# A two-layer transformer step on one core: the order of work at five norm boundaries, two modulation sums and the spatial gating

## What is computed

```python
for i in range(2):
    mod = c_act @ ada_w[i] + ada_b[i]                       # six vectors of 1024 for each layer
    sh1, sc1, g1, sh2, sc2, g2 = split(mod, 6)
    h = rmsnorm(x, norm_g[i, 0]) * (1.0 + sc1) + sh1
    y = mlstm_mixer(h, ...) if i == 0 else sgu_mixer(h, ...)
    x = x + g1 * rmsnorm(y, norm_g[i, 1])
    h = rmsnorm(x, norm_g[i, 2]) * (1.0 + sc2) + sh2
    y = square(relu(h @ ffn_w1[i])) @ ffn_w2[i]
    x = x + g2 * rmsnorm(y, norm_g[i, 3])
...
def sgu_mixer(h, ...):
    u, v = split(gelu(h @ w_in + b_in), 2)
    v = layernorm(v)
    sv = einsum('gts,bnsgc->bntgc', tril(ws), v in groups) + bs    # 16 groups of 128 features
    return (u * sv) @ w_out
```

## Time and profile before

| | us |
|---|---|
| median of three runs | 2238.09 |
| lowest and highest of them | 2231.41 and 2239.53 |
| the profiled execution's own time | 2227.2 |
| its span in the trace | 2225.4 |
| what lies around the span | 1.8 |

### The profile page before, as it was taken

One profiled execution on the slowest core, in us unless ns is written; L12 is line 12 of the kernel. 1 busy time (PEld: TensorE's weight loads), 2 busy tenths in 40 slices (PEclk: granted clock), 3 DMA queues, 4 the chain that ended last, 5 costly groups with the idle time before them and its releaser, 6 DMA issues.

```text
span 2225.4 us, 29809 instructions
## 1 busy us (share of the span) xinstructions
PE 2123.7 (95%) x11614; PEld 1777.6 (80%) x11614; DVE 1230.6 (55%) x1994; ACT 826.0 (37%) x1229; POOL 95.9 (4%) x71
## 2 busy tenths in 40 slices
PE   6999879999999999999999999999999999999997
PEld 5897768888888998788888888886666689888886
DVE  4666667666667445647333336535557756535455
ACT  3433334334244322325342343336445534424243
POOL 0000010000001002401000000100000000000000
PEclk9999989999999999999999999999999999999999
DMA  9451314666551432231223323222012131222221
GB/s 293 152 190 48 110 56 159 203 210 196 194 188 59 151 96 91 79 114 57 76 95 95 112 91 96 63 69 85 1 48 77 47 112 60 94 95 94 95 85 67
DMA packets 224630, 239.34 MB, mean 108 GB/s; under 512 B 6642, under 2 KB 219021, under 8 KB 223877
## 3 DMA queue, kind: packets, MB, share of 16 engines
q1 hardware_dynamic: 182757, 193.73, 27.1%
q10 hardware_dynamic: 41760, 44.06, 6.0%
HBM read 230.81 MB, written 6.31 MB: 107 GB/s over the span
## 4 chain that ended last, share of the span: by engine, by line
PE 66%; issue 18%; DVE 7%; DMA 3%; ACT 3%; DVEq 1%; POOL 1%; SPq 1%; ACTq 0%; POOLq 0%
PE bank L546 43%; PE bank L1133 4%; PE bank L686 2%; DMA ada_raw<-in_ada_w 2%; PE bank L740 2%; PE bank L644 2%; DVE ada_acc L1722 2%; PE bank L1081 1%; PE bank L1070 1%; PE bank L1028 1%; PE bank L1058 1%; PE bank L1104 1%; PE bank L1116 1%; ACT w_hi L1201 1%; PE bank L611 1%
## 5 line engine op out<-in xcount | busy, mean ns | idle before, releaser
L1711 DVE TENSOR_TENSOR w_lo<-raw,w_hi 128x2048 fp32r<-128x2048 f32 x137 | 314.6, 2296 | 246.2 <-ACT w_hi L1201 246.1
L546 PE MATMUL bank<-h_hi,w_hi 128*128 128x512 f32 x1056 | 413.7, 392 | 0.0
L546 PE MATMUL bank<-h_hi,w_lo 128*128 128x512 f32 x1056 | 411.7, 390 | 0.0
L546 PE MATMUL bank<-h_lo,w_hi 128*128 128x512 f32 x1056 | 411.6, 390 | 0.0
L1201 ACT ACTIVATE w_hi<-raw 128x2048 fp32r<-128x2048 f32 x147 | 280.1, 1905 | 314.4 <-PE bank L546 308.1
L546 PE MATMUL bank<-g_hi,w_hi 128*128 128x512 f32 x688 | 271.3, 394 | 9.4 <-DVE g_lo L2498 5.1
L546 PE MATMUL bank<-g_hi,w_lo 128*128 128x512 f32 x688 | 269.6, 392 | 0.0
L546 PE MATMUL bank<-g_lo,w_hi 128*128 128x512 f32 x688 | 269.4, 392 | 0.0
L546 PEld LDWEIGHTS bank<-h_hi,w_lo 128*128 128x128 f32 x1056 | 198.7, 188 | 41.6
L546 PEld LDWEIGHTS bank<-h_lo,w_hi 128*128 128x128 f32 x1056 | 198.8, 188 | 41.1 <-issue 0.2
L546 PEld LDWEIGHTS bank<-h_hi,w_hi 128*128 128x128 f32 x1056 | 198.7, 188 | 40.7 <-issue 0.2
(11 more groups left out here) (415 smaller groups left out, 3668.9 us busy)
## 6 DMA issues: line engine op xcount, KB each, us to landing
raw<-in_ffn_w SPq DMA_DIRECT2D x64, 1024.0 KB, 5.2
ada_raw<-in_ada_w ACTq DMA_DIRECT2D x40, 1024.0 KB, 5.2
raw<-in_w_up SPq DMA_DIRECT2D x22, 1024.0 KB, 5.0
raw<-in_b_w_in SPq DMA_DIRECT2D x16, 1024.0 KB, 5.3
raw<-in_w_in SPq DMA_DIRECT2D x15, 1024.0 KB, 5.6
raw<-in_a_w_in SPq DMA_DIRECT2D x12, 1024.0 KB, 5.5
ada_head<-in_ada_w SPq DMA_DIRECT2D x8, 1024.0 KB, 11.8
raw<-in_b_w_out SPq DMA_DIRECT2D x8, 1024.0 KB, 5.2
```

The lines of the kernel that those rows point to most:

```text
L546: mm = pe.matmul(o, x, y, start=(k == 0 and j == 0), stop=(k == kc - 1 and j == 2))
L1711: dve.tensor_tensor(w_lo[s][:], raw[s][:], f32(w_hi[s][:]), ALU.subtract).then_inc(sem("split_done"), 1)
```

## The change

It has three parts.

**The boundaries.** In `last_pair` the sums and spreads of half 0 come earlier: `sums` at k = 3 of block 0 of the second half (was k = 5), the first `spread_half` at k = 7 of block 0 (was k = 2 of block 1), the two batches of `x_sums` behind block 1 and at k = 2 of block 2 (were behind block 2 and at k = 2 of block 3), the second `spread_half` at k = 6 of block 2 (was k = 7 of block 3). The fourth square of y is no longer added by DVE; PE sums it by itself from its own tile. `first_pair` runs half 0 with k outside and the four blocks inside (was two tiles one after the other), with the norm steps of half 1 at k = 1, 2, 4, 5, 6 and 7. `merge` takes blocks in pairs, with one addition of 512 columns for two, and POOL adds nothing more. DVE and ACT get a new order for all of this; among it, the low part of the second tile of the next phase is made in one piece ahead of `y_out` of block 2 (it was in two pieces behind `y_out` of block 3), and on ACT the high part stands ahead of the squares of blocks 1 to 3 (it was ahead of that of block 3 alone). out2 gets the shared parts of this.

**The modulation.** Pieces 16 and 17 are summed inside the mixer, behind chunks 0 and 1; their loads, and that of 18, are issued there. 18 and 19 are summed in the two a_out tiles, and `last_ada` waits for the bias alone.

**The gating.** The turned weights come two tiles earlier, the norm of v skips ahead of some low parts, and the 16 groups stand in fours behind each of the last four b_in blocks, on four banks. ACT rounds the gated groups only behind its last gelu. The first b_out tile runs with k outside and its two blocks inside.

```diff
@@ TensorE, last_pair
-                            if (half, m, k) == (1, 0, 5):
-                                sums(0, 9 * kb_, sqa)
-                            if (half, m, k) == (1, 1, 2):
-                                spread_half(0, 2 * kb_)
-                            if two and (half, m, k) == (1, 3, 2):
-                                x_sums(name, 0, range(4, KB))
-                            if two and (half, m, k) == (1, 3, 7):
-                                spread_half(0, 2 * kb_ + 1)
+                            if (half, m, k) == (1, 0, 3):
+                                sums(name, 0)
+                            if (half, m, k) == (1, 0, 7):
+                                spread_half(name, 0)
+                            if two and (half, m, k) == (1, 2, 2):
+                                x_sums(name, 0, (2, 3))
+                            if two and (half, m, k) == (1, 2, 6):
+                                spread_half(name, 0, True)
...
-                        if two and (half, m) == (1, 2):
-                            x_sums(name, 0, range(4))
+                        if two and (half, m) == (1, 1):
+                            x_sums(name, 0, (0, 1))
@@ TensorE, sums
+                for i, sq in enumerate([sqa, T[3]]):
+                    if i == 0:
+                        pe.wait_ge(sem(f"sq_ready{half}"), 5 * kb_ + 1)
+                    else:
+                        pe.wait_ge(sem("y_squared"), 12 * kb_ + 8 + 4 * half)
@@ TensorE, first_pair
+                for k in range(KB):
+                    norm_step(name, k)
+                    pe.wait_ge(sem("h_ready0"), 8 * BOUNDS[name] + k + 1)
+                    for m in range(4):
+                        step(0, m // 2, m % 2, k, bank[m], True)
@@ TensorE, around a_out
+            for i in range(2):
+                ada_mm(16 + i, i)
             pe.wait_ge(sem("mix_out"), 8 + 2)
             for i in range(2):
                 tile(t0 + i, i % 2, q0 + i // 2, g_hi, g_lo)
-                ada_mm(16 + i, i % 2)
+                ada_mm(18 + i, i)
...
             def last_ada():
-                for i in range(2, 4):
-                    ada_mm(16 + i, i % 2)
                 pe.wait_ge(sem("ada_added"), 1)
@@ TensorE, gating
-            pe.wait_ge(sem("ws_masked"), 4)
-            pe.wait_ge(sem("v_normed"), NC)
-            for g in range(NSGU):
-                if g >= 2:
-                    pe.wait_ge(sem("sgu_added"), g - 1)
...
+            def sgu(t, b):
+                i = 2 * (t - t0 - 14) + b
+                if i == 0:
+                    pe.wait_ge(sem("ws_masked"), 4)
+                    pe.wait_ge(sem("v_normed"), NC)
+                for g in range(4 * i, 4 * i + 4):
+                    if g >= 4:
+                        pe.wait_ge(sem("sgu_added"), g - 3)
...
+            for s in range(2):
+                tile(t0 + 14 + s, s, q0 + 7, h_hi, h_lo, after_block=sgu)
@@ ScalarE, boundary
                 split_next(0)
-                for m in range(3):
-                    y_square(m, y[m], hs[0])
-                split_next(1)
-                y_square(3, y[3], hs[0])
+                y_square(0, y[0], hs[0])
+                split_next(1)
+                for m in range(1, 4):
+                    y_square(m, y[m], hs[0])
@@ VectorE, boundary
                 y_out(0, 0)
                 rest_of(t2, 0, next_w[name][0], 1)
                 y_out(0, 1)
                 y_sum(0, 0)
+                rest_of(t2, 1, next_w[name][1], 1)
+                y_out(0, 2)
                 y_sum(0, 1)
-                y_out(0, 2)
                 y_sum(0, 2)
                 y_out(0, 3)
-                y_sum(0, 3)
-                rest_of(t2, 1, next_w[name][1], 2, lambda: variance(0, 9 * kb_ + 1))
-                diagonal(0, 2 * kb_)
-                spread_done(0, 2 * kb_)
+                variance(0)
+                diagonal(0)
+                spread_done(0)
...
+                    for i in range(4):
+                        merge(0, i)
+                    y_out(1, 0)
+                    y_out(1, 1)
                     y_sum(1, 0)
+                    variance(0, True)
...
@@ VectorE, mixer
+                    ada_sum(16, 0, ada_raw, (sem("ada_in"), 16 * 9))
                 if c == 1:
                     w_rest(4, 1)
+                    ada_sum(17, 1, ada_raw, (sem("ada_in"), 16 * 10))
@@ VectorE, gating
-                if g == 2:
-                    w_rest(u0 + 7, 1)
-                if 3 <= g <= 10:
-                    sgu_rest(g - 3)
+                if g == 7:
+                    w_rest(u0 + 7, 0)
+                if g >= 11:
+                    sgu_rest(g - 11)
+            for g in range(5, 8):
+                sgu_rest(g)
+            w_rest(u0 + 7, 1)
```

More of the change, by code:

```diff
@@ new lines, in x_sums @@
+            def x_sums(name, half, pairs):
+                kb_, o = BOUNDS[name], bank[norm_banks(name, half)[2]]
+                for i in pairs:
+                    pe.wait_ge(sem(f"sq_ready{half}"), 5 * kb_ + i + 2)
+                    for b in (2 * i, 2 * i + 1):
+                        for c in range(2):
+                            mm = pe.matmul(o[:, c:c + 1], xsq[:, b, c * P:c * P + P], ones[:, 0:1],
+                                           start=(b == 0 and c == 0), stop=(b == KB - 1 and c == 1), skip_group_check=True)
@@ L665, in first_pair, with norm_step, step @@
+            def norm_step(name, k):
+                if k == 1:
+                    sums(name, 1)
+                if k == 2:
+                    spread_half(name, 1)
+                if k in (4, 5):
+                    x_sums(name, 1, (k - 4,))
+                if k == 6:
+                    x_sums(name, 1, (2, 3))
+                if k == 7:
+                    spread_half(name, 1, True)
             def first_pair(name, t, q):
-                one_bank = name == "out2"
-                for half in range(2):
+                def step(half, s, b, k, o, last):
@@ L689, in first_pair @@
-                    if half == 0 and not one_bank:
-                        spread_half(1, 2 * BOUNDS[name] + 1)
+                    wh, wl = (w[:, k * 256 + b * P:k * 256 + b * P + P] for w in next_w[name][s])
+                    for j, (x, y) in enumerate([(wh, h_hi[:, k, hs]), (wh, h_lo[:, k, hs]), (wl, h_hi[:, k, hs])]):
+                        mm = pe.matmul(o[:, hs], x, y, start=(k == 0 and j == 0), stop=(k == KB - 1 and j == 2))
+                    if k == KB - 1 and last:
+                        mm.then_inc(sem("block_done" if half else "half_done"), 1)
@@ L977, in _ @@
+            for i in range(1, 6):
                 first = i < 4
                 tile(t0 + i, i % 2, q0 + i // 2, h_hi if first else g_hi, h_lo if first else g_lo,
-                     ready=[(sem("sgu_split"), 0 if first else 8)] if i in (0, 4) else None)
+                     ready=[(sem("sgu_split"), 8)] if i == 4 else None)
             last_pair("b_out", t0 + 6, q0 + 3, g_hi, g_lo)
@@ L1858, in boundary @@
                 if two:
-                    merge(0, range(KB))
-                    for m in range(3):
-                        y_out(1, m)
+                    for i in range(4):
+                        merge(0, i)
+                    y_out(1, 0)
+                    y_out(1, 1)
                     y_sum(1, 0)
+                    variance(0, True)
                     y_sum(1, 1)
-                    variance(0, 9 * kb_ + 9, 1)
-                    y_sum(1, 2)
-                    diagonal(0, 2 * kb_ + 1)
@@ L1867, in boundary @@
[L1867 to L1874 removed]
+                    diagonal(0, True)
@@ new lines, in boundary @@
+                    h_rest(0, 4)
+                    diagonal(1)
+                    h_rest(0, 5)
+                    spread_done(1)
+                    merge(1, 0)
+                    merge(1, 1)
+                    h_scale(0, 6)
+                    h_rest(0, 6)
+                    merge(1, 2)
+                    merge(1, 3)
+                    h_scale(0, 7)
+                    h_rest(0, 7)
+                    variance(1, True)
+                    diagonal(1, True)
+                    spread_done(1, True)
```

354 lines of the change are left out of this document (187 added, 167 removed).

## The result

| | before | after |
|---|---|---|
| median of eight runs each, us | 2230.8 | 2221.0 |
| lowest and highest | 2228.03 and 2239.53 | 2215.22 and 2222.61 |
| span of the profiled execution | 2225.4 | 2213.4 |

The ratio of after to before is 0.9943 (95% interval 0.9930 to 0.9955). Of 2230.8 us that is 12.7 us less (10.0 to 15.6); the forecast was 17.5 less. That the median landed within half a microsecond of the forecast time is partly luck: with eight runs the median of before is 2230.8, not 2238.09.

The account below looks back on a forecast made before the run. PE, busy for 95% of the span, bounds the kernel. a_out −15.3, ffn0 +.4, ffn1 +2.0, b_out −.9, out2 +4.3, gating −8.0 sum to −17.5 us, median 2220.6; own range 2212 to 2230, 80% range 2204 to 2238.

Parts of the forecast that it names:

- The waits at the first sums: Boundaries: PE waits for sums held up by the second tile's load, 4.6 us in ffn1, 4.9 in out2.
- The walk: ffn1's boundary: chain from the load's landing through ACT and DVE to the last square, 6.65 us, ending at 1375.0.
- Rival B: Boundaries: the load holds nothing up, four us less at each of five, sum −37.5, 2200.6 us; chance .07.
- The sum of each boundary: Net change forecast per boundary: ffn0 +.4, b_out −.9, ffn1 +2.0, out2 +4.3 us.
- The waits for h in `first_pair`: PE's waits for h after the sums, some 7 us in all, shrink to about 2.
- The modulation: Mixer and a_out: sums of pieces 16 and 17 cost nothing in DVE's idle time; a_out's 7.3 us wait goes.
- a_out = ffn1's level: a_out falls from 81.7 us to ffn1's new 66.4, −15.3; bounds −7 to −17.3.
- rival C: Boundaries: each new wait brings 10 us at half clock, 5 lost; +17.5 in all, 2238 us; chance .14.
- The prediction's own sign for C: Boundaries: forecast wrong if the clock is at 0.50 for over 7 us behind the waits at the sums.
- D: Boundaries: each new wait brings 16 us at 0.50, seven more lost at each of five, +35; 2255.6 us; chance .06.
- The gating: Last b_in blocks: 128 matmuls at .122 us run without waits, 15.6 us in place of 23.6, −8; bounds 0 and −8.
- rival E: Gating gains nothing: late ACT rounding and low parts make b_out's first tile wait; −9.5, 2228.6 us; chance .13.

Follow-up runs that it names:

- bounds_only: The kernel before with the boundaries' new order alone; ratio to before 1.0024, median 2240.1 us.
- hi_early: The kernel after with the second tile's low part alone moved back on DVE, ACT's order unchanged; ratio to before 0.9891, median 2209.3 us.
- late1: The kernel after with the second tile's low part back behind the last `y_out`, high part ahead of the last square; ratio to before 0.9824, median 2196.3 us.
- gate_only: The kernel before with the gating's part alone; ratio to before 0.9981, median 2230.5 us.
- late_bounds: The kernel before with the boundaries' new order alone and the two places of late1; ratio to before 0.9950, median 2221.1 us.
- late_spread: late1 with PE's first spread six matmuls later; ratio to before 0.9836, median 2197.4 us.
- pieces: The kernel after with the second tile's high and low part cut in halves, in the same places; ratio to before 0.9914, median 2213.2 us.
- late2: The kernel after with the second tile's high part behind all four squares, low part behind the first spread; ratio to before 0.9865, median 2203.7 us.

## Why the prediction was right, and where it was off

**The waits at the first sums** were the step on which the forecast differed from the plain reading of the diff, and it held: 4.6 forecast for ffn1 and 3.4 measured, 4.9 for out2 and 4.2 measured. The walk was long by .7 to 1.2 us, since in ffn1 the high part started 10.4 us behind the start of `last_pair` (1349.66 against 1339.28), not 10.7, and DVE's and ACT's handovers were shorter: 5.75 us from there to the sums, not 6.65. bounds_only, hi_early and late1 show the cause by taking it away in two steps. Rival B falls.

**The sum of each boundary** came out close (+.7, −.5, +2.4, +4.8 for +.4, −.9, +2.0, +4.3), but by two errors that cancel. The waits for h in `first_pair` shrank by more than I took: no wait over .7 us stands behind the sums in any boundary after, where I still had 1.2 at the spread and 2 in `first_pair`. And half clock took more: it rose from 1.9 to 5.3 us in ffn1, where I had one dip of 1.7, and from 0 to 3.3 in out2, where the sum has no dip at all.

**The modulation** did what was said in the mixer: the two sums run in 177.3 to 181.6 and 199.8 to 204.1, in DVE's idle time, and from 148 us to a_out's start both traces take 120.1 us. The wait of 7.3 us at `last_ada` is gone. The term a_out = ffn1's level was mis-sized: 70.4, not 66.4. Of the 4 us, .3 is ffn1's own miss, and most of the rest is the clock, .12 × 70.5 = 8.5 us against 5.3 in ffn1. Here rival C, half clock behind the new wait, was partly right. PE's wait at a_out's sums ends at 285.4; the first of three dips runs from 284.6 to 291.5, the second from 298.3 to 305.1, inside full work (6 us of each):

```profile
285.00:291.00 6.00, 5.57 (x24) 5.39 (x25) 1.33 (x5) 0.42 (x1) 0.69 (x1) 0.50 0.54 174
299.00:305.00 6.00, 6.00 (x27) 5.82 (x28) 2.62 (x7) 2.31 (x3) 0.69 (x1) 0.50 0.00 1
```

In every boundary the first dip begins within 2.2 us of the end of that wait, before or behind it. Over all five, half clock took 28.9 us, 8.5 more than before. C's 17.5 has to be set against what the forecast allowed, 3.6 us in each of four boundaries and none in out2: 14.4, so 14.5 more were counted, close to C. The prediction's own sign for C, over 7 us at 0.50 behind the waits, was there too if the pieces are added up: 17.1, 10.2, 13.7 and 10.2 us in the first four boundaries, 6.8 in out2, none of them over 6.8 at a stretch. The time did not follow: the five boundaries came out only 5.7 us over the forecast, since part of the half clock fell into waits, where it costs nothing, and the other waits shrank by more than I took. So C had the clock nearly right and the sum wrong, and the forecast the reverse, which is luck in part. D's 35 is far off.

**The gating** gave 9.4 for 8. The term that was mis-sized is the matmul's rate: .111 us from start to start, not .122 (128 × .111 = 14.2, not 15.6). The POOL and ACT chain (rival E) held nobody: PE is busy for all of the four blocks with their groups, and for all of b_out's first tile, which runs from 900.6 to 911.5 at 1.37 us a k.

```profile
869.00:901.00 32.00, 32.00 (x207) 28.93 (x206) 13.75 (x19) 7.67 (x12) 18.28 (x13) 1.00 0.21 70
901.00:935.00 34.00, 34.00 (x151) 28.13 (x150) 22.73 (x25) 12.34 (x14) 5.59 (x4) 1.00 0.28 93
```

**What stands outside the sum**: +2.0 us ahead of a_out. They are all there at 148 us, ahead of the first changed instruction. The first load, that of x, lets PE start at 10.44 us and not at 9.76, which is .7; the rest is there by 40 us, where the same code ran 17.1 us at half clock from 18.4 us on, and 10.2 us in two dips in the trace of before. That is no effect of the change; without it the traces differ by 14.0.

So the direction, the mechanism of the waits and the place of the loss were right, and the size was too large, in the traces by 5.5 us: 4.1 at a_out, most of it clock, 1.6 in the other four boundaries, and 2.0 ahead of the change, less 1.4 that the gating gave more and .9 elsewhere. The term that was mis-sized is half clock behind the waits: 14.4 us allowed and 28.9 counted. What the prediction did not see is what late1 shows: that its own stall was worth undoing, and for more than its length. The stalls of 21.4 us and their clock cost about 27 us together, 26.0 in the boundaries of the traces. Not tried was the other way out, to leave the early parts where they are and let PE ask for the sums later.

## What to carry to other kernels

In an engine that runs in written order, put the instruction that waits for a load behind all that others wait for, even if its own result is needed soon: here two such moves turned a boundary order that lost 5 us into one that gained 11, and the whole change from 0.9943 to 0.9824. Walk each request of the bottleneck engine back through the written order of the engines that feed it, up to a DMA's landing, before moving requests earlier. And read a stretch's clock beside its waits: as much time can hang on it as on the waits themselves.

## What the runs showed of the hardware

**The same wait, with half clock behind it and without.** In the mixer PE waits 1.05 us for DVE. In the trace of before the clock stays full behind it; in late1 it falls at 159.86, .45 us behind the wait's end, and stays at half for 10.2 us. PE at the end of that wait in before, then in late1:

```profile
157.03 0.49 PE L785 MATMUL bank<-v_tok,tmp 128*128 128x128 f32 x2 [1.05 <-DVEq L2077]
```

```profile
159.41 0.49 PE L810 MATMUL bank<-v_tok,tmp 128*128 128x128 f32 x2 [1.05 <-DVEq L2167]
```

The stretch from 160 to 170 us of late1, then of before, where the same instructions stand 2.4 us earlier:

```profile
160.00:170.00 10.00, 10.00 (x50) 9.37 (x50) 3.70 (x10) 2.44 (x4) 0.00 (x0) 0.50 0.01 2
```

```profile
160.00:170.00 10.00, 10.00 (x78) 8.19 (x79) 8.12 (x20) 2.65 (x5) 1.64 (x1) 1.00 0.01 2
```

PE is busy for 10 of 10 us in both. gate_only, bounds_only, late1, late_bounds and late_spread have this dip, each from .3 to .9 us behind the end of that wait; the other seven traces have the wait and not the dip, and no instruction up to there differs between them. It costs 4.7 us (from the first matmul behind the keys to the next transposes 24.3 us in late1, 19.5 in before). Runs of the kernel before differ by such things: of eighteen, the three shortest (2226.6 to 2229.8) have a mean clock of .978 to .981, the three longest (2238.6 to 2239.5) of .975 to .978. A profiled execution of 2227.2 us at .981 stood at the short end, which is why its median lay above it. Whether the dip in the mixer is chance or hangs on where code lies could not be told: each kernel has one trace.

**One trace is a poor witness of what waits do to the clock.** In the boundaries of the traces, less waiting did not always go with less half clock. hi_early has half the waits of the kernel after and 31 us of clock loss, not less than its 29; late_spread has hardly any left and 17, late1 a few of 1 us and 12. bounds_only, where PE is idle for 33 us in the boundaries, has the most, 39 us, but the kernel before, with 36 us idle, has 20. Over all runs of each kernel the order is clearer: the mean granted clock is .973 in bounds_only (nine runs), .975 in the kernel after (eight), .977 in pieces, .978 in hi_early, .979 in late2, .981 in late_spread and .982 in late1 (four each), and the kernel before has .977 to .978 on each of the three chips of these runs. What it lacks of 1, times the span, is 55 us in the kernel after, 50 in hi_early and 40 in late1: 16 us of the 25 by which the mean spans of late1 and the kernel after differ. So over these kernels shorter waits at the sums went with a higher mean clock, while a single boundary can't be forecast from its waits.

The Trainium skill's page "TensorE: Matmul & The Clock Gate", section HAM oscillation, gives the price of a throttled stretch as its time × (1 − 1.2/2.4). The mixer's dip agrees: late1 and before differ by 4.7 us there, and 10.2 × .5 is 5.1.
